# Sample attention: two neighbouring keys of a page to a partition, on every second partition

## The reference

```python
k_past = cache_k[l][page_table].reshape(bs, past_len, A_HEADS, A_HEAD_DIM)   # 8 x 64 pages of 128 keys, 8 heads x 64
v_past = cache_v[l][page_table].reshape(bs, past_len, A_HEADS, A_HEAD_DIM)
f_past = cache_logf[l][page_table].reshape(bs, past_len, A_HEADS)
...
cum_f = jnp.cumsum(logf_all, axis=1)
...
s = jnp.einsum('bqhd,bkhd->bhqk', qi, k, preferred_element_type=jnp.float32) * scale
s = s + fi.transpose(0, 2, 1)[..., :, None] - fk_t[..., None, :]
s = jnp.where(mask, s, -jnp.inf)
p = jax.nn.softmax(s, axis=-1)
return jnp.einsum('bhqk,bkhd->bqhd', p.astype(v.dtype), v)
```

## Time and profile before

| | |
|---|---|
| median of 3 runs | 3416.41 us |
| lowest to highest | 3414.99 to 3417.76 us |
| the profiled execution | 3416.05 us |
| its span | 3414.3 us |
| TensorE busy | 3175.8 us, 93% |
| VectorE, ScalarE, GpSimd busy | 1775.6, 1414.2, 1044.3 us |
| moved by DMA | 817.78 MB, mean 240 GB/s |

### The profile page before, as it was taken

One profiled execution on the slowest core, in us unless ns is written; L12 is line 12 of the kernel. 1 busy time (PEld: TensorE's weight loads), 2 busy tenths in 40 slices (PEclk: granted clock), 3 DMA queues, 4 the chain that ended last, 5 costly groups with the idle time before them and its releaser, 6 DMA issues. The chain is left out here.

```text
span 3414.3 us, 58799 instructions
## 1 busy us (share of the span) xinstructions
PE 3175.8 (93%) x20175; PEld 2455.5 (72%) x20175; DVE 1775.6 (52%) x3118; ACT 1414.2 (41%) x2928; POOL 1044.3 (31%) x991
## 2 busy tenths in 40 slices
PE   7899999999999999999799999888888887999998
PEld 6678887787788778888577777555555555778787
DVE  4425556787756565555566666244444444444432
ACT  4412223454622474654577777422332333211222
POOL 2511313244354535140378788300000000222100
PEclk9999999999999999999799999999999999999999
DMA  7878788788879787878412222699999999554322
GB/s 270 306 229 270 237 253 263 243 317 277 291 249 322 237 292 243 278 239 230 121 38 63 66 66 90 235 386 386 382 388 383 386 385 333 192 167 166 130 88 83
DMA packets 430462, 817.78 MB, mean 240 GB/s; under 512 B 98605, under 2 KB 120021, under 8 KB 430186
## 3 DMA queue, kind: packets, MB, share of 16 engines
q1 hardware_dynamic: 418130, 807.02, 70.1%
q10 hardware_dynamic: 11488, 5.11, 0.6%
q0 software_dynamic: 576, 2.10, 0.2%
HBM read 674.11 MB, written 132.67 MB: 236 GB/s over the span
## 5 line engine op out<-in xcount | busy, mean ns | idle before, releaser
L1495 PE MATMUL prj_z_ps<-prj_w_hi,prj_h_ring 128*128 128x512 f32 x1792 | 724.2, 404 | 12.4 <-DMA prj_h_ring<-hops_scratch 7.3
L1497 PE MATMUL prj_z_ps<-prj_w_hi,prj_h_ring 128*128 128x512 f32 x1792 | 703.6, 393 | 0.0
L1496 PE MATMUL prj_z_ps<-prj_w_lo,prj_h_ring 128*128 128x512 f32 x1792 | 701.7, 392 | 0.0
L1964 POOL TENSOR_TENSOR pa_p_lo<-pa_probs,pa_p_hi 128x512 fp32r<-128x512 f32 (+1 forms) x320 | 368.2, 1170 | 108.0 <-ACT pa_p_hi L1976 104.7
L1495 PEld LDWEIGHTS prj_z_ps<-prj_w_hi,prj_h_ring 128*128 128x128 f32 x1792 | 339.1, 189 | 82.7 <-issue 8.2
L1497 PEld LDWEIGHTS prj_z_ps<-prj_w_hi,prj_h_ring 128*128 128x128 f32 x1792 | 338.2, 189 | 74.9
L1496 PEld LDWEIGHTS prj_z_ps<-prj_w_lo,prj_h_ring 128*128 128x128 f32 x1792 | 339.2, 189 | 66.5
L2645 PE MATMUL sa_t_ps<-arena_ident,arena_k_raw 128*128 128x128 f32 x2048 | 278.7, 279 | 114.9 <-DMA arena_k_raw<-in_cache_k_dram 104.3
L2525 DVE COPY sa_kT<-sa_t_ps 128x512 f32<-128x512 f32 x256 | 177.1, 692 | 355.6 <-PE sa_t_ps L2645 348.0
L2645 PEld LDWEIGHTS sa_t_ps<-arena_ident,arena_k_raw 128*128 128x128 f32 x2048 | 223.5, 141 | 167.2 <-DMA arena_k_raw<-in_cache_k_dram 136.3
L2469 ACT COPY sa_kT<-sa_t_ps 128x512 f32<-128x512 f32 x256 | 150.1, 586 | 444.2 <-PE sa_t_ps L2645 421.2
(11 more groups left out here) (414 smaller groups left out, 6209.0 us busy)
## 6 DMA issues: line engine op xcount, KB each, us to landing
prj_h_ring<-hops_scratch SPq DMA_DIRECT2D x448, 512.0 KB, 4.5
arena_k_raw<-in_cache_k_dram SPq DMA_DIRECT2D x512, 256.0 KB, 5.7
shared_v_early<-in_cache_v_dram SPq DMA_DIRECT2D x260, 256.0 KB, 5.9
sa_v_late<-in_cache_v_dram SPq DMA_DIRECT2D x252, 256.0 KB, 6.0
z_scratch<-prj_z_sb SPq DMA_DIRECT2D x224, 256.0 KB, 5.6
prj_raw<-in_w_main_dram SPq DMA_DIRECT2D x104, 256.0 KB, 5.9
arena_mg<-z_scratch SPq DMA_DIRECT2D x48, 512.0 KB, 4.8
hops_scratch<-prj_h_ring SPq DMA_DIRECT2D x32, 512.0 KB, 5.8
```

The lines of the kernel that those rows point to most:

```text
L1495: pe.matmul(out, h[:, 0, k], hi, start=(k == 0), stop=False)
L1496: pe.matmul(out, h[:, 0, k], lo, start=False, stop=False)
L1497: mm = pe.matmul(out, h[:, 1, k], hi, start=False, stop=(k == HK - 1))
L1964: pool.tensor_tensor(p_lo[:, s % P_RING, 0:w], probs[:, s % P_RING, 0:w], p_hi[:, s % P_RING, 0:w].bitcast(F32), ALU.subtract).then_inc(pl ...
```

## The change

A view `pages_of` takes two neighbouring keys of a page together, 64 rows of 4 KB. Each page, of keys and of values, is loaded as those 64 rows onto every second partition: pages with even j onto the even partitions, with odd j onto the odd ones, so that two pages fill the 128 partitions with two rows of 512 floats each (`page_in`). Column block j of a slot then holds, on partition p, key 2 (p // 2) + j % 2 of page 2 (j // 2) + p % 2 of the chunk.

A turn gives columns in which two pages alternate. The copies of the keys read them with a step of two (`from_turn`) and write each page's 64 keys side by side (`to_keys`, `block_of`), so scores come in the order: which of the two keys, pair of pages, page in the pair, 64 pairs of keys. The exponential writes its result with a step of two, which brings the weights of a block back into the order of the partitions, and `turn_weights` takes its slices by `block_of`. The decay is kept in the order of the scores: two of the subtractions on VectorE write (and one reads) even and odd keys apart, `decay_past` holds a chunk to a row block of 16 x 512, `store_past` writes it with 8 transfers of 32 rows of pieces of 256 bytes instead of 2, and `load_d` reads 16 rows of 2 KB. `load_k` waits once for two pages.

```diff
@@ -37,6 +37,7 @@
 PAST_LEN, PAGE = 8192, 128
 N_PAGES = PAST_LEN // PAGE
 CHUNK_PAGES = 4
+KEYS_EACH = 2
 CHUNKS = N_PAGES // CHUNK_PAGES
 HEADS, HEAD_DIM = 8, 64
 D_A = HEADS * HEAD_DIM
@@ -161,6 +162,17 @@
     _, pages = nc.values_load_multi_w_load_instructions(x, engines=(mybir.EngineType.SP,), min_val=0, max_val=n_pool - 1,
                                                         skip_runtime_bounds_check_because="page_table holds numbers of pages of the pool")
     return pages
+
+
+def pages_of(cache):
+
+    return cache.rearrange("l n (k e) h d -> (l n) k (e h d)", e=KEYS_EACH)
+
+
+def page_in(ring, slot, j):
+
+    first = j // KEYS_EACH * KEYS_EACH
+    return ring[j % KEYS_EACH:P:KEYS_EACH, slot, first:first + KEYS_EACH].rearrange("p e x -> p (e x)")
 
 
 def make_identity(pool, ident, zeroed, ready):
@@ -1657,6 +1669,7 @@
     P_RING = 6
     TURNS = len(TURN_ORDER)
     IN_GROUP = P // N_PAGES
+    PAST_STORE = 2 * CHUNK_PAGES * 16
     with ExitStack() as stack:
         m = Pool(nc, stack, "pa")
         own_k, own_q, own_v = shared.k_aug, shared.q_aug, shared.v_own
@@ -1818,10 +1831,15 @@
                 sp.dma_start(both[B_HIGH[is_q], hh, at].bitcast(F32), one[0:HEAD_DIM, hh, at].bitcast(F32)).then_inc(copied, 16)
 
             def store_past(group):
-                pages = slice(group * P, (group + 1) * P)
+                chunks, wide = P // CHUNK_PAGES, HEADS * KEYS_EACH
                 sp.wait_ge(past_step, 3 * group + 3)
-                sp.dma_start(decay_past[pages, 0:HEADS], d_hi[:].bitcast(F32)).then_inc(past_stored, 16)
-                sp.dma_start(decay_past[pages, HEADS:2 * HEADS], cum[:]).then_inc(past_stored, 16)
+                dst = decay_past[group * chunks:(group + 1) * chunks].rearrange("c h (e a b k) -> c (h e) a b k", a=CHUNK_PAGES // KEYS_EACH,
+                                                                               e=KEYS_EACH, b=KEYS_EACH)
+                for j in range(CHUNK_PAGES):
+                    a, b = divmod(j, KEYS_EACH)
+                    for half, src in enumerate((d_hi[:].bitcast(F32), cum[:])):
+                        sp.dma_start(dst[:, half * wide:(half + 1) * wide, a, b], src[j:P:CHUNK_PAGES].rearrange(
+                            "c h (e k) -> c (h e) k", e=KEYS_EACH)).then_inc(past_stored, 16)
 
             def load(h):
                 if h >= 4:
@@ -1849,23 +1867,23 @@
                     sp.dma_start(arena.tok[0:SAMPLE, i], tokens).then_inc(arena.tok_loaded, 16)
                     sp.dma_start(arena.tok[SAMPLE:P, i], z[b, SEQ + SAMPLE:ROWS, :]).then_inc(arena.tok_loaded, 16)
                 sp.wait_ge(arena.table_loaded, 16)
-                k_view = cache_k.rearrange("l n k h d -> (l n) k (h d)")
+                k_view = pages_of(cache_k)
                 for g in range(ring):
                     pages = page_numbers(nc, arena.table[0:1, bass.ds(g * CHUNK_PAGES, CHUNK_PAGES)], k_view.shape[0])
                     for j in range(CHUNK_PAGES):
                         src = k_view[bass.ds(pages[j], 1)].rearrange("a k x -> (a k) x")
-                        sp.dma_start(arena.k_raw[:, g, j], src).then_inc(arena.k_loaded[g], 16)
+                        sp.dma_start(page_in(arena.k_raw, g, j), src).then_inc(arena.k_loaded[g], 16)
 
             def begin_values():
                 sp.wait_ge(turned, HEADS * TURNS)
                 sp.wait_ge(max_turned, HEADS * GROUPS)
                 sp.wait_ge(vlo_ready, 2 * HEADS)
-                v_view = cache_v.rearrange("l n k h d -> (l n) k (h d)")
+                v_view = pages_of(cache_v)
                 for g in range(arena.RING):
                     pages = page_numbers(nc, arena.table[0:1, bass.ds(g * CHUNK_PAGES, CHUNK_PAGES)], v_view.shape[0])
                     for j in range(CHUNK_PAGES):
                         src = v_view[bass.ds(pages[j], 1)].rearrange("a k x -> (a k) x")
-                        sp.dma_start(shared.v_early[:, g, j], src).then_inc(shared.v_loaded[g], 16)
+                        sp.dma_start(page_in(shared.v_early, g, j), src).then_inc(shared.v_loaded[g], 16)
 
             with nc.allow_non_contiguous_dma(reason="512 words"):
                 sp.dma_start(page_of[:], page_table.rearrange("(g s) n -> (s n) g", s=IN_GROUP)).then_inc(past_stored, 16)
@@ -1899,7 +1917,7 @@
 
             all_steps(SyncPart())
             sp.wait_ge(stored, 16 * (HEADS // 2 - 1 + GROUPS))
-            sp.wait_ge(past_stored, 16 + 32 * (HEADS // 2))
+            sp.wait_ge(past_stored, 16 + PAST_STORE * (HEADS // 2))
 
         @block.gpsimd
         def _(pool):
@@ -2066,13 +2084,21 @@
                     if g == 1:
                         if j == 0:
                             dve.wait_ge(gathered, pair * 16 + 16)
-                            dve.wait_ge(past_stored, pair * 32 + 16)
+                            dve.wait_ge(past_stored, pair * PAST_STORE + 16)
                         by_head = lf[:].rearrange("p (k h) -> p h k", h=HEADS)[:, j]
                         dve.tensor_tensor_scan(cum[:, j], by_head, by_head, 0.0, ALU.add, ALU.bypass).then_inc(scanned, 1)
                     if g < 2:
                         return
                     log_rest = lf[:].rearrange("p (h k) -> p h k", h=HEADS)
                     wide = rest[:].unsqueeze(2).broadcast_to([P, HEADS, PAGE])
+                    each = rest[:].unsqueeze(2).unsqueeze(3).broadcast_to([P, HEADS, PAGE // KEYS_EACH, KEYS_EACH])
+
+                    def in_turn(x):
+                        return x.rearrange("p h (k e) -> p h k e", e=KEYS_EACH)
+
+                    def apart(x):
+                        return x.rearrange("p h (e k) -> p h k e", e=KEYS_EACH)
+
                     if (g, j) == (2, 0):
                         dve.wait_ge(scanned, pair * HEADS + HEADS)
                         dve.tensor_copy(whole[:], cum[:, :, PAGE - 1]).then_inc(whole_ready, 1)
@@ -2083,10 +2109,10 @@
                         dve.wait_ge(rest_ready, pair + 1)
                         dve.tensor_tensor(log_rest, wide, cum[:], ALU.subtract).then_inc(past_step, 1)
                     if (g, j) == (3, 11):
-                        dve.tensor_tensor(d_hi[:], wide, cum[:], ALU.subtract).then_inc(past_step, 1)
+                        dve.tensor_tensor(apart(d_hi[:]), each, in_turn(cum[:]), ALU.subtract).then_inc(past_step, 1)
                     if (g, j) == (3, 13):
                         dve.wait_ge(past_step, pair * 3 + 2)
-                        dve.tensor_tensor(cum[:], log_rest, d_hi[:].bitcast(F32), ALU.subtract).then_inc(past_step, 1)
+                        dve.tensor_tensor(apart(cum[:]), in_turn(log_rest), apart(d_hi[:].bitcast(F32)), ALU.subtract).then_inc(past_step, 1)
 
                 def maximum(self, h, u):
                     i, c = u
@@ -2340,11 +2366,21 @@
         def heads_of(x):
             return x.rearrange("p (c k) -> p c k", c=PAIRS)
 
+        def from_turn(j):
+            return t_ps[:, j % 2].rearrange("p (c k b) -> p c b k", c=PAIRS, b=KEYS_EACH)
+
+        def to_keys(g, j):
+            return kT[:, g % 2, :, block_of(j)].rearrange("p c (b k) -> p c b k", b=KEYS_EACH)
+
         def quad(c):
             return slice(c * QUAD, (c + 1) * QUAD)
 
         def dims(c):
             return slice(c * PAIR_D, (c + 1) * PAIR_D)
+
+        def block_of(j):
+            at = j % KEYS_EACH * (CP // KEYS_EACH) + j // KEYS_EACH
+            return slice(at * PAGE, (at + 1) * PAGE)
 
         def new_rows(n, h):
             return y_a[SEQ + n * DEC_SEQ:SEQ + (n + 1) * DEC_SEQ, h * HEAD_DIM:(h + 1) * HEAD_DIM]
@@ -2361,26 +2397,27 @@
         def _(sp):
             sp.dma_start(lf_new[:], logf[SEQ:ROWS, :]).then_inc(new_loaded, 16)
             sp.wait_ge(table_loaded, 16)
-            k_view = cache_k.rearrange("l n k h d -> (l n) k (h d)")
-            v_view = cache_v.rearrange("l n k h d -> (l n) k (h d)")
+            k_view, v_view = pages_of(cache_k), pages_of(cache_v)
             n_pool = k_view.shape[0]
 
             def find(chunk):
                 return page_numbers(nc, table[0:1, bass.ds(chunk * CP, CP)], n_pool)
 
-            def page(at, j, dst, view, sem):
-                sp.dma_start(dst[:, j], view[bass.ds(at, 1)].rearrange("a k x -> (a k) x")).then_inc(sem, 16)
+            def page(at, dst, view, sem):
+                sp.dma_start(dst, view[bass.ds(at, 1)].rearrange("a k x -> (a k) x")).then_inc(sem, 16)
 
             def load_k(g, slot, pages):
                 for j in range(CP):
-                    sp.wait_ge(turned, (g - RING) * CP + (j + 1))
-                    page(pages[j], j, k_raw[:, slot], k_view, k_loaded[slot])
+                    if j % KEYS_EACH == 0:
+                        sp.wait_ge(turned, (g - RING) * CP + (j + KEYS_EACH))
+                    page(pages[j], page_in(k_raw, slot, j), k_view, k_loaded[slot])
 
             def load_v(w, slot, pages, first=False):
                 for j in range(CP):
```

(18 more changed lines are left out.)

## The result

The kernel after takes 3488.0 us (median of four runs, 3482.2 to 3496.2), the kernel before 3415.7 us (four runs, 3410.3 to 3417.8). The ratio is 1.0216, with a 95% interval of 1.0192 to 1.024: 72 us slower, where 22 us faster was forecast, and outside the range.

What follows compares the result with a forecast made beforehand. The prediction took the full DMA engines loading keys and values in sample attention as the bound. Terms: -27 (larger pieces) + 3 (every second partition) + 2 (subtractions) = -22 us, 3416.4 to 3394 us; range 3369 to 3480.

Steps and rivals of the forecast that it cites:

- What bounds the kernel now: Sample attention, 685 us: the full DMA engines set the pace at 5.55 us a chunk; faster loads win at most 103.6 us.
- The 4 KB pieces: Key and value loads in sample attention: larger pieces raise 384 to 400 GB/s, 27 us won (ends 10 and 47).
- Every second partition: Sample attention loads onto alternate partitions: 3 us of loss taken, ends 0 and 598 us.
- The bound of 205 GB/s: Bad end for alternate partitions, from 64-row transfers into neighbouring partitions: 598 us lost if all bytes went at that rate.
- The copies: ScalarE and VectorE copies from PSUM (586 and 692 ns) with a step of two: even a doubling costs nothing.
- the third rival: VectorE becomes the bound in sample attention through slower copies; at 2.5 us each, +55 us, 3471 us; chance 0.04.
- the fourth: Rival: the change makes no larger packets, a 4 KB piece moving as two; 3416 us; chance 0.15 together with first rival.
- The waits: load_k's single wait per page pair and SP's issues: no cost; 0.33 us an issue, 8 to a chunk, 2.7 of 5.33.
- The second rival: Engines crowd on the way into the partitions, 205 GB/s for some bytes; 15% of them gives 3480 us; chance 0.28.
- The weights of the past: Prompt attention: store_past's eight issues cost 0, the out-of-turn VectorE subtractions 2 us (bounds 0 and 13).
- The signs: Trace marks to tell the outcomes apart; GB/s below 384 at a DMA share near 1 was to mean the second rival.

Runs made afterwards that it cites:

- a second issuer: Kernel before, with GpSimd issuing the values' transfers from the seventh chunk on, SP only the keys': 3413.55 us, ratio to the kernel before 1.0003.
- plain subtractions: Kernel after, with the decays of the past stored as in the kernel before (two transfers instead of eight, plain VectorE subtractions): 3483.4 us, ratio 1.0203.
- after with GpSimd: Kernel after, with GpSimd issuing the values' transfers from the seventh chunk on, SP only the keys': timed 3398.95 us, ratio to the kernel before 0.9958.

## Why the prediction was wrong

**What bounds the kernel now: right.** Before, SP waits for buffers and a second issuer changes nothing (3413.55 us). But the view that showed it, 40 us of waits in 500, was also the view that showed how near the next bound was: 0.44 us for a chunk. I read its sign and not its size.

**The 4 KB pieces: right that the layout moves more, and roughly to size.** I took 400 GB/s and -27 us. With the issuing out of the way it is 398 GB/s, 685 x (1 - 384/398) = 24 us by the prediction's own formula, and 5.42 against 5.56 us for 123 chunks, 17 us, by the chunks; the whole program is 14.6 us under the kernel before with the same second issuer. That it is the pieces, and not something else in the layout, wasn't separated (see the packets of GpSimd's queue below).

**Every second partition: right in the main point.** 3 us taken; with 398 GB/s where 400 were assumed there is no room for more. The bound of 205 GB/s described the neighbouring halves.

**The copies: right.** 692 and 587 ns, no cost; VectorE was nowhere the bound, and the third rival falls. So does the fourth: q1's packets in the stage went from 103661 to 52241.

**The waits: this is the step that failed.** The price of the new issues on SP was put at nothing, and it is 1.1 us a chunk. "An issue takes SP 0.33 us, 8 to a chunk, 2.7 us of 5.33" carried a duration over to a transfer of another shape, and left out what SP does between issues. The sum should have been 4.77 us of a chunk's 5.56, and then 0.14 us more for each of eight issues has 0.44 us to hide in at most. I bounded the 64-row transfers' speed in the DMA engines by the earlier trace rows and never their price on SP, though it stands in the same fence: two 64-row issues of 1.22 us, 0.61 each (with two pieces to a partition). As the upper bound, 8 x (0.61 - 0.33) = 2.2 us on the 5.56 - 0.44 = 5.12 us that SP is at work, it gives 7.3 us a chunk and (7.3 - 5.56) x 123 = 214 us; half of it gives 6.2 us and 79 us. The trace of before even had the right price: line 2842's 64-row load of 2 KB rows, 0.47 us beside 0.32, shown above. With it a chunk comes to 5.12 + 8 x (0.47 - 0.33) = 6.24 us and the loop to 84 us more; 67 were measured. No rival held it. The second rival had nearly the right time (3480 us) from the wrong mechanism; that is luck.

**The weights of the past: too low, if anything.** The eight issues take 0.63 to 0.65 us each, one of them 1.68, and hold SP for 6.4 us after the last group of pages, and the first key load of the prompt's ring starts at 2114.7 instead of 2107.4 us; as said, nothing waits for it. The subtractions grew from 2132 and 1215 to 2954 and 2283 ns, inside the bound of a doubling, 7.6 us of VectorE in all. Taken were 2 us; the runs point to about 4 (3488.0 against 3483.4, intervals overlapping), perhaps through GpSimd: it is busy 402.2 us from 1645 to 2160, against 396.4 before and 396.7 with plain subtractions. Why its work lengthens beside these wasn't tried.

**The signs.** "GB/s below 384 at a DMA share still near 1" was to mean crowding. It didn't: with SP as the bound the share stayed at 0.98. Taking bytes away (0.58, same time), and giving SP less to do, showed that the engines weren't the bound.

## What to carry to other kernels

Before you reshape a transfer, add up the issuing queue for one round of the loop, lookups and gaps included, and compare the sum with the round; the queue's waits for free buffers were all the slack that it had here. Price the new shape's issue by a row of that shape, as you would its speed. And a DMA share near 1 doesn't say that the DMA engines bound: ask whether the queue that feeds them ever waits; where it doesn't, move part of it to an engine whose instructions nobody is waiting for.

## What the chip showed that was not expected

- A transfer of half as many partitions was dearer to issue on SP: 332 ns for 128, 474 for 64, 542 for 64 in two pieces each; 286 for 8, so it doesn't go on rising. The Trainium skill ("Perfetto Trace Analysis", What "DMA-bound" means) says that large descriptors are what helps when the issuing sequencer is the limit. Here half as many descriptors of twice the size made each issue 142 ns longer; the measurement decides.
- GpSimd's issue took 536 ns in both shapes, and its queue carried the 2 KB rows of the kernel before in 4 KB packets, by the bytes of one: 28545 packets for 93.56 MB, 3278 bytes each with the small ones at the ends, as in the kernel after (171.23 MB in 52241), where SP's queue needs 51667 for 94.08 MB. So the control with GpSimd had half of its bytes in large packets already, and still moved 383 GB/s; the whole of the step to 398 came with the change's layout. That makes larger packets by themselves a doubtful cause of it. The DMA queues of that control, 2250 to 2750:

```profile
q1 hardware_dynamic: 51667, 94.08, 51.4%
q0 software_dynamic: 28545, 93.56, 49.3%
```

- TensorE's granted clock, 1.00 in the stage before, is 0.96 in the mean of the kernel after, so in part of it TensorE ran at 1.2 and not 2.4 GHz, as its waits for keys grew from 76.5 to 103.5 us in 500. It still waited for the keys afterwards, which is why I take it to cost nothing. No run was made to test it, but the kernel before with GpSimd also has 0.96 in the stage, and takes as long as the kernel before.
- A DMA share of 0.98 is compatible with engines that could move more, since a packet's time isn't fixed. In the kernel after 4 KB packets and their ends took 95.3% of 8000 us for 171.23 MB, 44.5 us for a MB; with a full queue (SP's queue of after with GpSimd) 50.0% for 97.68 MB, 41.0 us. At that rate the kernel after's bytes would take 88% (an estimate from these rows). What makes the packets longer no run shows.
